# The order of seven products, four PSUM banks for them, and four banks for the second weight matrix

## The chip, the cores and the metric

The kernel runs as one program on one core of one Trainium2 chip. The metric is the device time of one execution in microseconds (us). The kernel is written with one instruction stream for each engine and with semaphores between them: TensorE (PE) multiplies, VectorE (DVE) and ScalarE (ACT) read the results in PSUM, GpSimd (POOL) works only in SBUF, and SyncE (SP) issues all DMAs. PSUM has 8 banks here, `ps[:, 0..7, :]`, each with room for 512 float32 values in a partition.

## The reference

One inference step of one layer. The stage that the change touches is the SwiGLU feed-forward at the end of the layer:

```python
def residual_tail(h, oa, ob, g_out_a, g_out_b, w_out, g_ffn, w_gate, w_up, w_down):
    mixed = jnp.concatenate([rmsnorm(oa, g_out_a), rmsnorm(ob, g_out_b)], axis=-1)
    h = h + mixed @ w_out
    u = rmsnorm(h, g_ffn)
    return h + (jax.nn.silu(u @ w_gate) * (u @ w_up)) @ w_down
```

There are 1024 prompt frames and 32 sample frames (1056 tokens), `D_MODEL` is 1024 and `D_FF` is 2816, which is 22 blocks of 128. All is float32. Ahead of this stage stand a combined input projection, two kinds of attention (forgetting attention and sliding-window attention) and the output projection; the change leaves those alone.

## The kernel before

**Three matmuls for one.** Each float32 matrix is kept as a high part (rounded to float32r) and a low part (the rest). `product` (L734 to L737) issues three matmuls: high by high (L735), weights high by data low (L736), weights low by data high (L737). For each operand ACT copies the high part and DVE subtracts to get the low part.

**Seven products for eight.** In the feed-forward the two matrices gate and up, and the two halves of the tokens, are treated as a 2 by 2 block product and computed with seven block products in place of eight (Strassen's scheme in Winograd's form). The weights' sums and differences are made by POOL (`weight_sums`, L2436 to L2451: four in each step), those of the input by `input_sum` once per pass, in place, in the staged columns `st_a` (pass 0, POOL) or `st_b` (pass 1, POOL and DVE). `fu0` to `fu6` are the seven inputs, each as `hi` and `lo`; `fw` has 9 slots for split weights.

**Passes and steps.** Pass 0 takes 512 tokens (halves of 256), pass 1 takes 544 (halves of 272). Each pass has 22 steps `g`, one for each 128 columns of `w_gate` and `w_up`; steps 0 to 21 are pass 0, steps 22 to 43 pass 1. `SETS` is 44 and `NF` 22. In a step PE issues products P0 to P6 (`ffn_product`, 12 matmuls each). Product number e = 7g + i is written to bank `e % SPARE`, and `SPARE` is 6. Between products stand the four pieces D0 to D3 of the product with `w_down` of the step before (`down_piece`): order P0 D0 P1 P2 D1 P3 P4 D2 P5 P6 D3. In pass 0 a piece is one group of 512 columns, in pass 1 two groups of 272. Groups go to banks 6 and 7 in turn, as `down_banks` (L445) lays out; the turned rows (`turn_half`, PE transposes of `y` for the output) use the same two.

**What DVE does with the products.** ACT copies P0 to `x1` (`copy_out`). DVE then has seven places in each step, at fixed points of its program, where it adds a bank (L2100 and L2109). Before the change they are: P1 to the first gate, P2 to `x2`, P4 to `x3`, P5 to the second gate, P3 to both `x2` and `x3` (`add_fourth`, L2102, two instructions), and, at the start of the next step, P6 to `x2`. In the text these are called place 1, place 2, place 3, place 4, the double place and place 6. Between them DVE splits weights (L2055), multiplies the gates (L2119), splits the hidden values (L2126) and `w_down` (L2134), and adds the groups of D0 to D3 to `y` (L2149, or L2146 in the first unit of a pass).

**What holds PE.** Before product e, PE waits (`bank_read`, L1136) until the product SPARE back has been read, that is for a place of DVE (or `f_x`, the copy by ACT). Before a group, it waits until the last user of its bank has been added (`down_bank_free`, L1163), until the hidden values are split (`f_hl`) and until the weights are (`dw_lo`). In steps 0 and 22 the inputs `fu` change too, so products wait for `u_lo`.

**The pass change.** In step 21 DVE and ACT also make the inputs of pass 1 (`input_hi`, `input_lo` L2084, `input_sum` L2074 to L2078), and in step 22 the last two of them. In steps 24 and 25 the first four result rows are turned and added to the residual (`add_half`, L2160); in steps 26 to 29 DVE normalises them (`out_row`, L2181, after the double place and ahead of place 6). The last units are computed after step 43, with the rows 4 to 8.

Of the kernel before, what the change touches and what calls it, by code (L numbers as in the profile page):

```python
# [421 lines left out]
U_ORDER = (0, 1, 2, 3, 5, 6, 4)  # L422
# [41 lines left out]
def build(nc, x_p, x_s, ck_fox, cv_fox, cl_fox, ck_swa, cv_swa, rel_bias, g_attn, w_in, b_forget, sinks,  # L464
# [17 lines left out]
    with ExitStack() as ctx:  # L482
# [231 lines left out]
        U_FROM = ((0, 0), (1, 0), (0, 0), (0, 1), (0, 1), (1, 1), (1, 0))  # L714
        U_SUMS = (0, 0, 2, 1, 4, 0, 3)
# [17 lines left out]
        def _(pe):  # L733
# [402 lines left out]
            def bank_read(g, i):  # L1136
# [3 lines left out]
                if i == 3:  # L1140
                    return S["f_p7"], 2 * g + 2
                return S["f_add"], 5 * g + {1: 1, 2: 2, 4: 3, 5: 4, 6: 5}[i]

            def ffn_product(g, i):
# [4 lines left out]
                if g % NF == 0:  # L1149
                    pe.wait_ge(S["u_lo"], 7 * p + U_ORDER.index(i) + 1)  # L1150
# [85 lines left out]
        def _(act):  # L1236
# [413 lines left out]
            for s in range(1, TILES + 1):  # L1650
# [11 lines left out]
                if s >= 6:  # L1662
                    for i in U_ORDER[2 * (s - 6):2 * (s - 6) + 2]:
# [6 lines left out]
            for g in range(SETS):  # L1670
                if g >= 1:
                    silu(g - 1, 1)
                if g == NF:
                    input_hi(1, 6)
                copy_out(g)
                if g == NF:
                    input_hi(1, 4)
# [20 lines left out]
                if g == NF - 1:  # L1698
                    input_hi(1, 5)
# [19 lines left out]
        def _(dve):  # L1719
# [343 lines left out]
            def input_sum(p, x):  # L2063
# [4 lines left out]
                else:  # L2068
                    dve.wait_ge(S["u_sum"], 4 * p + x)
                    dve.wait_ge(S["u_lo"], 7 * p + (1, 2, 4)[x - 1])  # L2070
# [6 lines left out]
                else:  # L2077
                    dve.tensor_tensor(b12, b22, b11, ALU.subtract).then_inc(S["u_sum"], 1)  # L2078

            def input_lo(p, i):  # L2080

                n = HALF_OF[p]
                dve.wait_ge(S["u_hi"], 7 * p + U_ORDER.index(i) + 1)
# [3 lines left out]
            def add_bank(g, i):  # L2087
# [4 lines left out]
                dst, src = {1: (gate0, first), 2: (x2, first), 4: (x3, x2), 5: (gate1, x3), 6: (x2, x2)}[i]  # L2092
# [3 lines left out]
                elif i < 6:  # L2096
                    dve.wait_ge(S["f_add"], 5 * g + i - 2)
# [4 lines left out]
            def add_fourth(g):  # L2102

                n, par = HALF_OF[pass_of(g)], g % 2
                dve.wait_ge(S["f_pe"], 7 * g + 4)
                for x in range(2):
                    dve.wait_ge(S["f_add"], 5 * g + 3 + x)
                    part = x23[par][:, x, 0:n]
                    dve.tensor_tensor(part, part, bank((7 * g + 3) % SPARE, n), ALU.add).then_inc(S["f_p7"], 1)  # L2109
# [75 lines left out]
            for s in range(1, TILES + 1):  # L2185
# [9 lines left out]
                if s >= 6:  # L2195
                    for i in U_ORDER[2 * (s - 6):2 * (s - 6) + 2]:
# [8 lines left out]
            for g in range(SETS):  # L2205
# [6 lines left out]
                if g == NF:  # L2212
                    input_lo(1, 6)
# [6 lines left out]
                if g == NF:  # L2220
                    input_lo(1, 4)
# [19 lines left out]
                if g == NF - 1:  # L2241
                    input_lo(1, 2)
                if g == NF + 2:
# [4 lines left out]
                add_bank(g, 4)  # L2248
# [3 lines left out]
                if g == NF - 1:  # L2252
                    input_lo(1, 3)
                    input_sum(1, 3)
# [590 lines left out]
```

## Time and profile before

| | us |
|---|---|
| median of three executions | 1372.18 |
| lowest, highest | 1371.8, 1377.6 |
| profiled execution, its own time | 1376.14 |
| its span | 1374.2 |
| PE busy | 1320.5 (96%) |
| DVE busy | 948.3 (69%) |
| ACT busy | 661.1 (48%) |
| POOL busy | 526.3 (38%) |

The span is the time from the first to the last instruction in the trace. A view of the trace gives places in it as microseconds from the span's start. In the page's row of 40 slices PE reads 9 nearly everywhere, and DVE reads 9 or 8 from the 26th slice on, which is the feed-forward; so the two engines run side by side there. Ends of matmuls are modelled, and a matmul's own 0.28 us overlaps with the next one's, so a product's length is read from start to start.

### The profile page before, as it was taken

What the parts mean: (1) busy time and instruction counts of PE and PEld (TensorE: products, weight loads), DVE (VectorE), ACT (ScalarE), POOL (GpSimd) and SP (SyncE); (2) the same over time, 40 slices, a digit from 0 to 9 for tenths busy, and PEclk for the clock granted to TensorE, in tenths of its full rate; (3) what the DMA queues carried; (4) which work ended last, traced back from release to release, by engine and by line L of the source; (5) the groups of instructions that cost most, each with busy time, mean ns of one, the idle gap of its engine ahead of it and who ended that gap; (6) DMA issues with size and microseconds to landing.
All of it is one profiled execution on the core that took longest, in us unless ns stands there. A gap on an engine that the chain in (4) does not pass through costs nothing.

```text
span 1374.2 us, 25904 instructions
## 1 busy us (share of the span) xinstructions
PE 1320.5 (96%) x9497; PEld 1198.1 (87%) x9497; DVE 948.3 (69%) x1899; ACT 661.1 (48%) x1418; POOL 526.3 (38%) x499
## 2 busy tenths in 40 slices
PE   7999999999999899999999999999999999999996
PEld 5989888788887678777999999998889999999996
DVE  6346653333232433478999999999998998899976
ACT  6346564756455553367443444445454433334432
POOL 3045552545435232125544444444343444434400
PEclk9999999999999999999999999999999999999999
DMA  7631115312112344563343333332532444333311
GB/s 207 109 81 36 33 52 162 101 32 63 63 45 78 96 170 137 172 207 107 94 122 108 93 106 111 103 98 81 166 92 78 124 124 155 96 105 93 93 51 65
DMA packets 167235, 141.10 MB, mean 103 GB/s; under 512 B 17280, under 2 KB 143328, under 8 KB 166600
## 3 DMA queue, kind: packets, MB, share of 16 engines
q1 hardware_dynamic: 167112, 139.46, 35.0%
q8 instruction: 77, 1.26, 0.4%
q14 instruction: 46, 0.38, 0.1%
HBM read 116.00 MB, written 23.54 MB: 102 GB/s over the span
## 4 chain that ended last, share of the span: by engine, by line
PE 80%; DVE 10%; issue 5%; ACT 3%; DMA 2%; POOL 1%; SPq 0%; DVEq 0%; ACTq 0%
PE ps L735 24%; PE ps L737 23%; PE ps L736 23%; PE ps L939 3%; DVE fw L2055 2%; PE ps L869 1%; DMA cb<-c_scratch 1%; PE ps L951 1%; PE ps L816 1%; PE ps L1028 1%; DVE y L2149 1%; PE ps L907 1%; DMA ob<-o_scratch 1%; DVE ps L1850 1%; DVE h_lo L2126 1%
## 5 line engine op out<-in xcount | busy, mean ns | idle before, releaser
L2446 POOL TENSOR_TENSOR sums<-fraw 128x512 f32<-128x512 f32 x44 | 73.3, 1666 | 402.8 <-DMA fraw<-in_w_up 381.3
L735 PE MATMUL ps<-h_hi,dw 128*128 128x272 f32 (+1 forms) x512 | 168.0, 328 | 8.9 <-DVE y L2149 6.4
L2055 DVE TENSOR_TENSOR fw<-sums,fw 128x512 fp32r<-128x512 f32 x176 | 172.5, 999 | 0.0
L2402 POOL TENSOR_TENSOR pl_x<-sp_x,ph_x 128x512 fp32r<-128x512 f32 (+5 forms) x120 | 102.3, 866 | 169.8 <-ACT sp_x L1428 168.5
L737 PE MATMUL ps<-h_hi,dw 128*128 128x272 f32 (+1 forms) x512 | 166.8, 326 | 0.0
L736 PE MATMUL ps<-h_lo,dw 128*128 128x272 f32 (+1 forms) x512 | 165.9, 324 | 0.0
L1632 ACT ACTIVATE sg<-sg 128x256 f32<-128x256 f32 (+1 forms) x88 | 37.5, 426 | 230.9 <-DVE sg L2100 230.6
L2149 DVE TENSOR_TENSOR y<-y,ps 128x272 f32<-128x272 f32 (+1 forms) x240 | 120.4, 516 | 25.0 <-PE ps L737 22.4
L1592 ACT ACTIVATE fw<-sums 128x512 fp32r<-128x512 f32 x176 | 104.5, 622 | 41.6 <-PE ps L737 39.2
L735 PEld LDWEIGHTS ps<-h_hi,dw 128*128 128x128 f32 x512 | 96.4, 188 | 15.2 <-issue 10.8
L1427 ACT ACTIVATE ph_x<-ps,negc 128x512 fp32r<-128x512 f32 (+5 forms) x120 | 63.0, 525 | 84.2 <-PE ps L951 84.2
L737 PEld LDWEIGHTS ps<-h_hi,dw 128*128 128x128 f32 x512 | 96.6, 189 | 7.2
L736 PEld LDWEIGHTS ps<-h_lo,dw 128*128 128x128 f32 x512 | 96.7, 189 | 3.9
L1592 ACT ACTIVATE fw<-fraw 128x512 fp32r<-128x512 f32 x132 | 78.3, 626 | 30.6 <-PE ps L737 30.6
L2055 DVE TENSOR_TENSOR fw<-fraw,fw 128x512 fp32r<-128x512 f32 x132 | 91.1, 717 | 0.0
L1884 DVE CUSTOM_DVE_ANT_0 ps<-ps,cb 128x512 f32<-128x512 f32 (+4 forms) x72 | 40.1, 597 | 71.1 <-PE ps L916 42.9
L2449 POOL TENSOR_TENSOR sums<-fraw 128x512 f32<-128x512 f32 x44 | 82.7, 1880 | 0.0
L2451 POOL TENSOR_TENSOR sums<-fraw,sums 128x512 f32<-128x512 f32 x44 | 78.6, 1787 | 0.0
L2134 DVE TENSOR_TENSOR dw<-draw,dw 128x1024 fp32r<-128x1024 f32 x43 | 78.4, 1822 | 0.0
L735 PE MATMUL ps<-u_hi,cw1hi 128*128 128x384 f32 (+1 forms) x216 | 75.4, 349 | 0.0
L735 PE MATMUL ps<-u_hi,cw0hi 128*128 128x384 f32 (+1 forms) x216 | 75.0, 347 | 0.0
L736 PE MATMUL ps<-u_lo,cw1hi 128*128 128x384 f32 (+1 forms) x216 | 70.0, 324 | 0.0
(358 smaller groups left out, 4428.7 us busy)
## 6 DMA issues: line engine op xcount, KB each, us to landing
fraw<-in_w_gate SPq DMA_DIRECT2D x44, 512.0 KB, 4.0
fraw<-in_w_up SPq DMA_DIRECT2D x44, 512.0 KB, 5.3
draw<-in_w_down SPq DMA_DIRECT2D x44, 512.0 KB, 3.6
x_scratch<-xb SPq DMA_DIRECT2D x16, 512.0 KB, 2.9
raw<-in_w_in SPq DMA_DIRECT2D x14, 512.0 KB, 4.0
cb<-c_scratch SPq DMA_DIRECT2D x4, 1312.0 KB, 7.2
xt<-in_x_prompt SPq DMA_DIRECT2D x8, 512.0 KB, 4.2
out<-outb SPq DMA_DIRECT2D x16, 256.0 KB, 3.1
```

Source lines behind the costliest of these rows:

```text
L735: pe.matmul(out, wh, xh, start=start, stop=False)
L736: pe.matmul(out, wh, xl, start=False, stop=False)
L737: return pe.matmul(out, wl, xh, start=False, stop=stop)
L1427: act.activation(ph_x[2 * (v % 2) + h][0:rows, 0:n], ps[0:rows, b + h, 0:n], ACT.Exp, bias=decay, scale=-1.0)
L1592: act.activation(fw[e % SLOTS][:, 0, :, :], weight_block(g, i), ACT.Copy).then_inc(S["fw_hi"], 1)
L2055: dve.tensor_tensor(lo, weight_block(g, i), hi.bitcast(F32), ALU.subtract).then_inc(S["fw_lo"], 1)
L2134: dve.tensor_tensor(down_weight(n)[:, 1, :, :], draw[:], down_weight(n)[:, 0, :, :].bitcast(F32), ALU.subtract)\
L2149: dve.tensor_tensor(dst, dst, bank(DOWN_BANK["group", at], width), ALU.add).then_inc(S["y_add"], 1)
L2402: pool.tensor_tensor(pl_x[at][0:rows, 0:n], sp_x[at][0:rows, 0:n], ph_x[at][0:rows, 0:n].bitcast(F32), ALU.subtract).then_inc(S["x_pl"], 1)
L2446: pool.tensor_tensor(s1, a21, a22, ALU.add).then_inc(S["fw_sum"], 1)
L2449: pool.tensor_tensor(s3, a11, a21, ALU.subtract).then_inc(S["fw_sum"], 1)
L2451: pool.tensor_tensor(s4, a12, s2, ALU.subtract).then_inc(S["fw_sum"], 1)
```

## The change

Three things are changed together.

1. The products P3, P4 and P5 are renumbered. What was P3 (added to both sums) is now P5; what was P4 is now P3, and what was P5 is now P4. So DVE's places are now: P1, P2, P3, P4, P5 (double, `add_both`), P6. The places themselves stay where they were in DVE's program, with the same operands and sizes.
2. `SPARE` goes from 6 to 4: products use banks 0 to 3. The groups and the turned rows use banks 4 to 7.
3. The inputs and weight sums follow the new numbers: `U_FROM`, `U_SUMS`, `SUM_OF`, `SUM_DONE`, `U_ORDER`, the order of two of POOL's four sums, and in step 21 the last `input_sum`, which stands ahead of `down_lo` now and not after the fourth input.

```diff
-SPARE = 6
+SPARE = 4
-SUM_OF = {2: 0, 3: 1, 4: 2, 5: 3}
-SUM_DONE = {2: 2, 3: 3, 4: 1, 5: 4}
+SUM_OF = {2: 0, 5: 1, 3: 2, 4: 3}
+SUM_DONE = {2: 2, 3: 1, 4: 3, 5: 4}
-U_ORDER = (0, 1, 2, 3, 5, 6, 4)
+U_ORDER = ((0, 1, 2, 4, 5, 3, 6), (0, 1, 2, 3, 4, 5, 6))
...
-            uses += [("turn", 4 + t, 6 + t % 2) for t in range(4)]
-        uses.append(("group", at, 6 if n == NF + 1 else 6 + at % 2))
+            uses += [("turn", 4 + t, 4 + t % 4) for t in range(4)]
+        uses.append(("group", at, 4 + at % 3 if n == NF + 1 else 4 + at % 4))
...
-        U_FROM = ((0, 0), (1, 0), (0, 0), (0, 1), (0, 1), (1, 1), (1, 0))
-        U_SUMS = (0, 0, 2, 1, 4, 0, 3)
+        U_FROM = ((0, 0), (1, 0), (0, 0), (0, 0), (1, 1), (0, 1), (1, 0))
+        U_SUMS = (0, 0, 2, 4, 0, 1, 3)
...
-                if i == 3:
+                if i == 5:
                     return S["f_p7"], 2 * g + 2
-                return S["f_add"], 5 * g + {1: 1, 2: 2, 4: 3, 5: 4, 6: 5}[i]
+                return S["f_add"], 5 * g + min(i, 5)
...
-                dst, src = {1: (gate0, first), 2: (x2, first), 4: (x3, x2), 5: (gate1, x3), 6: (x2, x2)}[i]
+                dst, src = {1: (gate0, first), 2: (x2, first), 3: (x3, x2), 4: (gate1, x3), 6: (x2, x2)}[i]
...
-            def add_fourth(g):
+            def add_both(g):
...
-                dve.wait_ge(S["f_pe"], 7 * g + 4)
+                dve.wait_ge(S["f_pe"], 7 * g + 6)
...
                 if g == NF - 1:
                     input_lo(1, 2)
+                    input_sum(1, 3)
...
-                add_bank(g, 4)
+                add_bank(g, 3)
...
                 if g == NF - 1:
                     input_lo(1, 3)
-                    input_sum(1, 3)
...
-                add_bank(g, 5)
-                add_fourth(g)
+                add_bank(g, 4)
+                add_both(g)
```

On PE nothing moves: the same matmuls stand in the same order, and only what they wait for differs. Here is P4 of step 2, its first matmul before (-) and now (+); `fw_186` is a weight slot, `f_add` counts places 1 to 4 and 6, and `f_x` the copies by ACT.

```order
 L736 MATMUL ps<-fu3lo,fw_195 128x256
 L737 MATMUL ps<-fu3hi,fw_195 128x256
-L735 MATMUL ps<-fu4hi,fw_186 128x256 [waits f_add,fw_lo]
+L735 MATMUL ps<-fu4hi,fw_186 128x256 [waits f_x,fw_lo]
 L736 MATMUL ps<-fu4lo,fw_186 128x256
 L737 MATMUL ps<-fu4hi,fw_186 128x256
```

P4 waited for the bank of the fifth product of the step before (place 4) and now waits for P0 of its own step. With `bank_read` worked out for all seven, P0 now waits for place 3 of the step before (it was place 1), P1 for place 4 (it was place 2), P2 for the double place (as before), P3 for place 6 (it was place 3), P4 for ACT's copy, P5 for place 1 and P6 for place 2 of its own step.

On PE again, a group of `w_down` in step 25, behind the four turned rows of that step; `e_r` counts the turned rows that DVE has added.

```order
 L736 MATMUL ps<-fu5lo,fw_186 128x272
 L737 MATMUL ps<-fu5hi,fw_186 128x272
-L735 MATMUL ps<-h_hi_190,dw_215 128x272 [waits y_add,dw_lo,f_hl]
+L735 MATMUL ps<-h_hi_190,dw_215 128x272 [waits e_r,dw_lo,f_hl]
 L736 MATMUL ps<-h_lo_191,dw_215 128x272
 L737 MATMUL ps<-h_hi_190,dw_215 128x272
```

This is the third group, behind P5, and the fourth has the same difference: it waited for the first group's addition and now waits for a turned row, since the four turned rows have four banks. The first two groups waited for the last two of the four turned rows of that step and now wait for the first two.

On DVE, in step 21 (the pass change), from the third input on; `fu2lo` to `fu5lo` are inputs of pass 1 and `st_b` the staged columns.

```order
 L2084 TENSOR_TENSOR fu2lo<-st_b,fu2hi 128x1088
+L2078 TENSOR_TENSOR st_b<-st_b 128x4x272
 L2134 TENSOR_TENSOR dw_216<-draw,dw_216 128x1024
 L2100 TENSOR_TENSOR x_1_221<-x_1_221,ps 128x256
 L2149 TENSOR_TENSOR y<-y,ps 128x512
 L2084 TENSOR_TENSOR fu3lo<-st_b,fu3hi 128x1088
-L2078 TENSOR_TENSOR st_b<-st_b 128x4x272
 L2055 TENSOR_TENSOR fw_213<-sums_217,fw_213 128x512
 L2055 TENSOR_TENSOR fw_192<-sums_217,fw_192 128x512
 L2100 TENSOR_TENSOR sg_214<-x_1_221,ps 128x256
```

The sum has moved ahead of four instructions, of which one is place 3 (the row of L2100 on `x_1`); the last row shown, L2100 on `sg`, is place 4. The number of instructions on each engine is the same.

## Rows read from the trace of the kernel before

**Rows 1.** The page: busy time of each engine, and the chain by engine.
```profile
PE 1320.5 (96%) x9497; PEld 1198.1 (87%) x9497; DVE 948.3 (69%) x1899; ACT 661.1 (48%) x1418; POOL 526.3 (38%) x499
...
PE 80%; DVE 10%; issue 5%; ACT 3%; DMA 2%; POOL 1%; SPq 0%; DVEq 0%; ACTq 0%
```

**Rows 2.** Stretches: length, busy of PE, PEld, DVE, ACT, POOL, clock, DMA, GB/s.
```profile
800.00:900.00 100.00, 100.00 (x706) 93.50 (x706) 91.82 (x151) 43.14 (x85) 44.43 (x26) 1.00 0.36 104
938.00:972.00 34.00, 30.05 (x192) 27.17 (x192) 33.69 (x44) 16.38 (x26) 11.39 (x7) 0.95 0.21 63
1023.29:1034.63 11.34, 9.71 (x75) 9.28 (x74) 8.43 (x15) 8.28 (x13) 5.63 (x4) 1.00 0.13 48
1051.26:1068.94 17.68, 16.85 (x134) 16.66 (x134) 16.81 (x30) 6.85 (x13) 6.76 (x4) 1.00 0.39 106
1051.26:1120.72 69.46, 67.29 (x530) 66.63 (x530) 64.95 (x114) 27.39 (x52) 27.23 (x16) 1.00 0.41 119
1203.83:1220.44 16.61, 16.61 (x134) 16.61 (x134) 15.22 (x27) 6.80 (x13) 6.67 (x4) 1.00 0.36 97
1344.87:1361.60 16.73, 15.02 (x113) 14.00 (x112) 11.43 (x22) 4.07 (x7) 0.00 (x0) 1.00 0.07 27
```

**Rows 3.** Waits of PE from 640 to 1374: total us, times, longest.
```profile
PE ps L735 <- DVE y L2149: 6.9, 8, 2.7
```

**Rows 4.** DVE in order of time, end of step 12: start, us, what.
```profile
815.05 0.41 DVE L2100 TENSOR_TENSOR x<-x,ps 128x256 f32<-128x256 f32 x1
...
818.50 0.41 DVE L2100 TENSOR_TENSOR sg<-x,ps 128x256 f32<-128x256 f32 x1
```

**Rows 5.** PE in order of time, products P0 and P1 of step 13.
```profile
818.29 0.28 PE L735 MATMUL ps<-fu0hi,fw 128*128 128x256 f32 x1
...
821.09 0.28 PE L735 MATMUL ps<-fu1hi,fw 128*128 128x256 f32 x1
```

**Rows 6.** DVE in order of time, end of step 1.
```profile
653.02 0.41 DVE L2100 TENSOR_TENSOR x<-x,ps 128x256 f32<-128x256 f32 x1
...
656.42 0.41 DVE L2100 TENSOR_TENSOR sg<-x,ps 128x256 f32<-128x256 f32 x1
```

**Rows 7.** PE in order of time, P1 and P2 of step 2.
```profile
654.42 0.28 PE L735 MATMUL ps<-fu1hi,fw 128*128 128x256 f32 x1
...
657.63 0.36 PE L735 MATMUL ps<-fu2hi,fw 128*128 128x256 f32 x1 [1.64 <-DVE x L2109]
```

**Rows 8.** DVE in order of time, the pass change (steps 21 and 22).
```profile
959.77 0.41 DVE L2100 TENSOR_TENSOR x<-x,ps 128x256 f32<-128x256 f32 x1
...
962.08 1.29 DVE L2078 TENSOR_TENSOR st_b<-st_b 128x1088 f32<-128x1088 f32 x1
...
964.49 0.42 DVE L2100 TENSOR_TENSOR sg<-x,ps 128x256 f32<-128x256 f32 x1
```

**Rows 9.** PE in order of time, the pass change: P0 of step 22, D0, P4.
```profile
956.56 0.29 PE L735 MATMUL ps<-fu0hi,fw 128*128 128x272 f32 x1
...
960.92 0.47 PE L735 MATMUL ps<-h_hi,dw 128*128 128x512 f32 x1 [2.68 <-DVE y L2149]
...
971.75 0.36 PE L735 MATMUL ps<-fu4hi,fw 128*128 128x272 f32 x1 [0.78 <-issue]
```

**Rows 10.** PE in order of time, second and third group of step 25.
```profile
1025.57 0.36 PE L735 MATMUL ps<-h_hi,dw 128*128 128x272 f32 x1 [1.34 <-DVE hrow L2160]
...
1028.36 0.36 PE L735 MATMUL ps<-h_hi,dw 128*128 128x272 f32 x1 [0.29 <-DVE y L2146]
```

**Rows 11.** PE in order of time, after step 43: groups at 1337 and the last turns.
```profile
1337.73 0.36 PE L735 MATMUL ps<-h_hi,dw 128*128 128x272 f32 x1 [0.83 <-DVE y L2149]
...
1362.08 2.84 PE L1204 MATMUL ps<-ident,y 128*128 128x128 f32 x24 [0.98 <-DVE y L2149]
```

**Rows 12.** DVE in order of time, one row of step 26 and one of the end.
```profile
1051.58 1.28 DVE L2181 SCALAR_TENSOR_TENSOR hrow<-hrow,small,g_fin 128x1024 f32<-128x1024 f32 x1
...
1341.49 1.22 DVE L2134 TENSOR_TENSOR dw<-draw,dw 128x1024 fp32r<-128x1024 f32 x1
```

More of the change, by code:

```diff
@@ L1149, in ffn_product @@
                 if g % NF == 0:
-                    pe.wait_ge(S["u_lo"], 7 * p + U_ORDER.index(i) + 1)
+                    pe.wait_ge(S["u_lo"], 7 * p + U_ORDER[p].index(i) + 1)
                 if e >= SPARE:
@@ L1662, in _ @@
                 if s >= 6:
-                    for i in U_ORDER[2 * (s - 6):2 * (s - 6) + 2]:
+                    for i in U_ORDER[0][2 * (s - 6):2 * (s - 6) + 2]:
                         input_hi(0, i)
@@ L1673, in _ @@
                 if g == NF:
-                    input_hi(1, 6)
+                    input_hi(1, 5)
                 copy_out(g)
                 if g == NF:
-                    input_hi(1, 4)
+                    input_hi(1, 6)
                 if g == NF - 1:
@@ L1698, in _ @@
                 if g == NF - 1:
-                    input_hi(1, 5)
+                    input_hi(1, 4)
                 if g == NF + 3:
@@ L2069, in input_sum @@
                     dve.wait_ge(S["u_sum"], 4 * p + x)
-                    dve.wait_ge(S["u_lo"], 7 * p + (1, 2, 4)[x - 1])
+                    dve.wait_ge(S["u_lo"], 7 * p + x)
                 if x == 0:
@@ L2095, in add_bank @@
                     dve.wait_ge(S["f_x"], g + 1)
-                elif i < 6:
-                    dve.wait_ge(S["f_add"], 5 * g + i - 2)
+                elif i < 5:
+                    dve.wait_ge(S["f_add"], 5 * g + i - 1)
                 else:
@@ L2108, in add_fourth @@
                     part = x23[par][:, x, 0:n]
-                    dve.tensor_tensor(part, part, bank((7 * g + 3) % SPARE, n), ALU.add).then_inc(S["f_p7"], 1)
+                    dve.tensor_tensor(part, part, bank((7 * g + 5) % SPARE, n), ALU.add).then_inc(S["f_p7"], 1)
             def gated(g, j):
@@ L2195, in _ @@
                 if s >= 6:
-                    for i in U_ORDER[2 * (s - 6):2 * (s - 6) + 2]:
+                    for i in U_ORDER[0][2 * (s - 6):2 * (s - 6) + 2]:
                         input_lo(0, i)
@@ L2212, in _ @@
                 if g == NF:
-                    input_lo(1, 6)
+                    input_lo(1, 5)
                 weights_lo(g, 0)
@@ L2220, in _ @@
                 if g == NF:
-                    input_lo(1, 4)
+                    input_lo(1, 6)
                 pieces_added(g, 0)
@@ L2265, in _ @@
                 if g == NF - 1:
-                    input_lo(1, 5)
+                    input_lo(1, 4)
                 if g == NF + 4:
@@ L2439, in weight_sums @@
                 a22 = fraw[g % 2][:, 1, 4:8, :]
-                s1, s2, s3, s4 = (sums[g % 2][:, SUM_OF[i], :, :] for i in (4, 2, 3, 5))
+                s1, s2, s3, s4 = (sums[g % 2][:, SUM_OF[i], :, :] for i in (3, 2, 5, 4))
                 pool.wait_ge(S[f"fw_in{g % 2}"], 32 * (g // 2 + 1))
@@ L2459, in input_sum @@
                     pool.wait_ge(S["u_sum"], 4 * p + x)
-                    pool.wait_ge(S["u_lo"], 7 * p + (1, 2, 4)[x - 1])
+                    pool.wait_ge(S["u_lo"], 7 * p + x)
                 if x == 0:
```

8 lines of the change are left out of this document (4 added, 4 removed).

## The prediction, made before the changed kernel ran

> **What bounds the kernel now.** I read the page first: PE is busy for 1320.5 us and the chain that ends last is PE for 80% of the span and DVE for 10% [rows 1]. Then the view of stretches over the feed-forward. In a stretch of pass 0 PE is busy for all of its 100 us and DVE for 91.8, and in a step of pass 1 (16.61 us) PE again for all of it and DVE for 15.22 [rows 2]. So in the steady steps PE sets the pace, and what the change does there can only add. In a few stretches PE has gaps: at the pass change (30.05 busy of 34.00), in step 25 (9.71 of 11.34), in steps 26 to 29, and after the last step (15.02 of 16.73) [rows 2]. Third, the view of waits says what PE waited for: most of all additions to `y`, 6.9 us in 8 waits [rows 3]. An addition to `y` frees a bank of a group, and there are two of those. A gain can come only from these gaps. Last, I laid the starts of products beside the ends of DVE's places, since with four banks each product waits for a later place than before.
>
> **Steady steps: cost nothing.** P0 now waits for place 3 of the step before, P1 for place 4. Place 3 of step 12 ends at 815.05 + 0.41 = 815.46 and P0 of step 13 starts at 818.29; place 4 ends at 818.91 and P1 starts at 821.09 [rows 4, 5]. The margins are 2.8 and 2.2 us. P2 waits for the double place as before, and P3 to P6 wait for places that lie further ahead of them. The additions keep their sizes and their places in DVE's program, and each now reads a product that PE finishes at the same point or earlier, the double place apart: its product is P5 now, which ends a product and a group (together 2.80, the distance of the two rows in [rows 5]) ahead of P0's 818.29, at 815.5, well before the double place, which stands behind place 4. So: 0, and upwards whatever a DVE that runs over 2.2 us later would cost (the second rival).
>
> **The start: +0.3.** In the first steps DVE is far behind, since there is no `w_down` work on PE yet. Place 3 of step 1 ends at 653.43 and place 4 at 656.83 [rows 6]. P1 of step 2 started at 654.42, which is now too early by 2.4 us: it starts at about 656.9, and P2 a product (1.4 us, half of that 2.80) later, at 658.3, in place of 657.63, where P2 already ended a wait of 1.64 us for the double place [rows 7]. So most of the new wait takes the place of an old one, and 0.7 is left. Against it, step 0 gets shorter, because the input that is split last is now needed by P6 and no longer by P4, and with it step 1 on DVE can start a little earlier. No row prices that. Ends: -0.5 and +1.5; I take +0.3, near the 0.7 of the rows.
>
> **The pass change: +0.1.** This is the place where the change bites. P0 of step 22 started at 956.56, and place 3 of step 21 stood at 959.77, with the last sum of 1.29 us behind it at 962.08 [rows 8, 9]. The sum is now ahead of place 3, so place 3 ends at 959.77 + 1.2 + 0.4 = 961.4, and P0 starts there, 4.9 us later than before. But D0 behind it was waiting until 960.92 anyway (2.68 us, for an addition to `y` that now has a bank of its own), and P4 waited until 971.75 for the input that DVE split last [rows 9]; that input now belongs to P6. From 961.5 on PE has P0, D0, P1, P2, D1, P3 ahead of P4: four products of 12 x 0.126 = 1.51 (the pace is worked out under step 25) and two groups of 1.38, 8.8 us, so P4 could start at 970.3, and with P1 held until place 4 (964.49 + 0.42 = 964.9 [rows 8]) at 970.8, 1 us early. The clock takes that back. The stretch from 938 to 972 has a mean of 0.95 of the full clock [rows 2], which is 34 x 0.05 / 0.5 = 3.4 us at the lower of the two levels, 1.2 GHz. The same 3.4 us now lie wholly on PE's work, and cost 1.7 us, less the 0.5 that P1 would have waited: P4 at 972.0 and so +0.1 against 971.75 or a little more. Ends: -1.0 (no low stretch on the path) and +1.8 (a second low stretch of that length, as PE's gap grows from 2.7 to about 5 us).
> The Trainium skill (TensorE: Matmul & The Clock Gate, HAM oscillation) says that PE falls back to the half clock after it has stood idle, so a longer gap can cost a second low stretch. By that rule the sum would end 1.7 us higher. The trace agrees that one such stretch follows the gap; how it is with a longer gap no row here shows.
>
> **Step 25: -2.3.** Behind the four turned rows the second group waited 1.34 us for the last turned row's addition and the third another 0.29 [rows 10]. With four banks it is the fourth group that needs the last turned row's bank; it comes a product and three groups after the first, at 1023.29 + 1.51 + 2.27 = 1027.1, and the addition was over at 1025.57. The stretch from 1023.29 to 1034.63 then has only its 72 matmuls. A steady step holds 132 in 16.61 us, 0.126 each, so 72 take 9.06 us and not 11.34 [rows 2]: -2.3. Ends: 0 (DVE gives nothing back) and -2.3.
>
> **Steps 26 to 29: -3.0.** In each of these DVE has a row of the result of 1.28 us ahead of place 6 [rows 12], and with it the additions of D3 come late; D0 of the next step needed their bank. The four steps take 69.46 us, the first of them 17.68 [rows 2]. Four steady steps are 66.44. With four banks D0 waits for D2 of the step before, which DVE adds ahead of place 4 and so before its result row. What is late next is place 3 for P0, and that stands ahead of the result row too. DVE itself has 64.95 us of work in these four steps [rows 2], under 66.44, so it can follow. Ends: 0 and -3.0.
>
> **After step 43: -2.8.** The third group there waited for an addition to `y`, and started at 1337.73 and not at once, 1.0 us late [rows 11]. Then DVE splits the last part of `w_down` until 1341.49 + 1.22 = 1342.7 [rows 12]; the ninth group needs it and started at 1344.87, since groups were held by two banks on the way. It can start at 1342.9, -2.0. From there PE had 16.73 us, with 15.02 busy, DVE 11.43 [rows 2]: 1.7 us of gaps, which two more banks close, but for what DVE's last additions and two result rows hold up; I take half, -0.8. Sum -2.8. The last turns, at 1362.08 [rows 11], and all behind them move along. Ends: -1.0 (only the first wait) and -3.1.
>
> **Other edits: 0.** POOL's two sums are exchanged; POOL mostly waits for weights, with 44.43 us busy of 100 [rows 2]. ACT makes the fourth input later in step 21, as it now needs the last sum, but DVE has `w_down`, place 3 and an addition between that sum and its own part of that input. The DMAs are the same.
>
> **Sum.** 0 + 0.3 + 0.1 - 2.3 - 3.0 - 2.8 = -7.7. On the profiled execution's own 1376.14 us that is 1368.4. That execution is 4.0 us above the median of the three runs, 1372.18, and nothing in the page says why; I take the difference off the median: 1364.5 us.
>
> **Rivals.**
> 1. *DVE takes the gain back.* In pass 1 with four banks PE is no longer held at D0, but DVE was busy for 16.81 us in step 26, more than the 16.61 of a steady step [rows 2]. If it is the true bound of steps 25 to 29, the 5.3 us there are not gained but wait at a later product. For it: DVE's busy time. Against: 64.95 in four steps, and the gaps of DVE in step 25 (8.43 busy of 11.34 [rows 2]). Then -2.4, 1369.8 us.
> 2. *Four product banks are too few* (the other side). The margin of P1 is 2.2 us in the steady steps [rows 4, 5]. If DVE, with a different meeting of its splits with POOL's sums, runs later than that, P1 waits in each step; decided from a lag of 2.2 us on. By 0.5 us in each of the 37 steps outside the places above it is +18.5, with the gains 1383. For it: DVE is busy 91.8% [rows 2]. Against: it has 8% to catch up with, and steps of equal work have had that margin.
> 3. *The two bad places cost their full price:* the start +1.5, the pass change +1.8 with a second low stretch and a P0 that no longer hides behind D0. Then 1364.5 + 2.9 = 1367.4.
> 4. *The new order does more:* the start -0.5, the pass change -1.0, the end -3.1: 1362.3. It goes with the forecast.
>
> **How the numbers follow.** Forecast (with 4): 0.65; rival 1: 0.16; rival 3: 0.14; rival 2: 0.05. 0.5% is about what a measurement of this kernel can tell from no change, 6.9 us: faster means under 1365.3. The forecast's own range is 1361.5 to 1366.5, since medians of three runs scatter too, and about 0.83 of it lies under 1365.3: faster 0.54 and 0.11 of it the same; rivals 1 and 3 are the same but for 0.01: same 0.41; slower 0.05. The range of 8 in 10 takes in most of rivals 1 and 3: 1361.5 to 1370.
>
> **What would show it.** The waits of PE for `y` go from 6.9 us to below 1; steps 26 to 29 take 16.6 us each; the stretch of step 25 takes about 9; the waits that appear are for place 4 in step 2 and for place 3 in step 22, of some 5 us; the span from the first turn after the last group to the end stays as it is. Wrong would be: products that wait in steady steps, a DVE without gaps in steps 25 to 30, or more than one low stretch of the clock near 961.

## The result, and the profile after

The changed kernel took 1367.74 us (median of 8 runs, 1366.13 to 1370.4), the kernel before in the same comparison 1375.62 us (8 runs, 1371.8 to 1379.0). The ratio is 0.9947 with a 95% interval from 0.9933 to 0.996: 7.3 us faster (7.9 by the two medians). The prediction was 1364.5 us, as 7.7 us less than a base of 1372.18 us.

The page of the changed kernel, busy time and chain, answers to [rows 1]:

```profile
PE 1316.1 (96%) x9497; PEld 1197.0 (88%) x9497; DVE 944.3 (69%) x1899; ACT 660.2 (48%) x1418; POOL 520.9 (38%) x499
...
PE 84%; DVE 8%; issue 3%; ACT 3%; DMA 2%; POOL 1%; SPq 0%; DVEq 0%; ACTq 0%
```

PE has 84% of the chain where it had 80%. Its span is 1364.3 us. Then the stretches that answer to [rows 2], with the same columns (length, busy of PE, PEld, DVE, ACT, POOL, clock, DMA, GB/s): a steady stretch of pass 0, the pass change, step 25 from its first group on, step 26, steps 26 to 29, and the end from the ninth group behind D3 to the last addition to `y`.

```profile
800.00:900.00 100.00, 100.00 (x704) 93.43 (x703) 90.89 (x154) 45.63 (x89) 40.97 (x25) 1.00 0.38 106
938.00:972.00 34.00, 28.89 (x189) 26.72 (x189) 33.69 (x49) 18.32 (x30) 8.68 (x5) 0.95 0.27 74
1020.61:1029.69 9.08, 9.08 (x74) 9.08 (x73) 8.46 (x15) 8.28 (x13) 5.79 (x4) 1.00 0.21 61
1046.33:1062.95 16.62, 16.62 (x134) 16.62 (x133) 15.50 (x31) 6.96 (x14) 6.32 (x4) 1.00 0.43 128
1046.33:1112.77 66.44, 66.44 (x530) 66.44 (x529) 61.51 (x116) 27.56 (x53) 26.10 (x16) 1.00 0.44 128
1334.91:1350.46 15.55, 13.96 (x114) 13.63 (x112) 11.68 (x24) 4.06 (x7) 0.00 (x0) 1.00 0.07 29
```

The reader is to see where PE's gaps went. Step 25 has 9.08 us and not 11.34, steps 26 to 29 have 66.44 and not 69.46, both without a gap. The pass change still has one (28.89 busy of 34.00), and so has the end (13.96 of 15.55).

What PE waits for, in the changed kernel from 630 us on (total us, times, longest), answers to [rows 3]:

```profile
PE ps L735 <- DVE x L2100: 6.1, 2, 5.1
PE ps L1204 <- DVE y L2149: 2.1, 1, 2.1
PE ps L735 <- DVE sg L2100: 1.9, 2, 1.7
```

No group waits for an addition to `y` any more (before: 6.9 us in 8 waits). Place 3 (`x`: P0 of step 22 with 5.1 us, and P0 of step 2 with 1.0) and place 4 (`sg`: P1 of step 2 with 1.7) have taken their stead, and the last turns wait 2.1 us.

Laid beside each other from the first product of the feed-forward (P0 of step 0) to the end, the two profiled executions differ as follows. The last column is the changed kernel profiled a second time, `c1_changed_again`, told of below.

| stretch | predicted | changed | again |
|---|---|---|---|
| ahead of P0 of step 0 | | -3.3 | -3.5 |
| start (to P0 of step 3) | +0.3 | +0.8 | +1.9 |
| steps 3 to 20 | 0 | 0.0 | 0.0 |
| pass change (P0 of step 21 to P0 of step 23) | +0.1 | +0.1 | +1.1 |
| steps 23 and 24 | 0 | -0.2 | -0.5 |
| step 25 | -2.3 | -2.2 | -2.2 |
| steps 26 to 29 | -3.0 | -3.0 | -3.0 |
| steps 30 to 42 | 0 | 0.0 | 0.0 |
| end (from P0 of step 43) | -2.8 | -2.0 | -3.3 |
| from P0 of step 0 on | -7.7 | -6.5 | -5.9 |

The first row lies ahead of all that was changed: in all twelve other profiled executions of this study P0 of step 0 came 1.3 to 3.5 us earlier than in the one of before, `e4_before_rows_later`, which has the same order and banks, among them (1.8 us). So it is taken to be the execution's and not the change's.

### The profile page after: what moved, and what is told of

The parts are those of the page before. It is cut to its first block, busy times and chain, and to the rows that moved or that the text cites. A ratio compares the mean times of both kernels' runs of the same rounds, so it can differ in the third digit from the quotient of the medians.

```text
span 1364.3 us, 25904 instructions
## 1 busy us (share of the span) xinstructions
PE 1316.1 (96%) x9497; PEld 1197.0 (88%) x9497; DVE 944.3 (69%) x1899; ACT 660.2 (48%) x1418; POOL 520.9 (38%) x499
## 3 DMA queue, kind: packets, MB, share of 16 engines
q8 instruction: 78, 1.28, 0.4%
## 4 chain that ended last, share of the span: by engine, by line
PE 84%; DVE 8%; issue 3%; ACT 3%; DMA 2%; POOL 1%; SPq 0%; DVEq 0%; ACTq 0%
PE ps L735 25%; PE ps L737 24%; PE ps L736 24%; PE ps L939 3%; DVE fw L2055 2%; PE ps L869 1%; DMA cb<-c_scratch 1%; PE ps L951 1%; PE ps L816 1%; PE ps L1028 1%; PE ps L907 1%; DVE ps L1850 1%; DMA ob<-o_scratch 1%; ACT sp_x L1428 0%; ACT raw L1551 0%
## 5 line engine op out<-in xcount | busy, mean ns | idle before, releaser
L2446 POOL TENSOR_TENSOR sums<-fraw 128x512 f32<-128x512 f32 x44 | 72.0, 1636 | 402.5 <-DMA fraw<-in_w_up 397.8
L2055 DVE TENSOR_TENSOR fw<-sums,fw 128x512 fp32r<-128x512 f32 x176 | 175.0, 1013 | 0.0
L2055 DVE TENSOR_TENSOR fw<-fraw,fw 128x512 fp32r<-128x512 f32 x132 | 89.7, 706 | 0.0
L2451 POOL TENSOR_TENSOR sums<-fraw 128x512 f32<-128x512 f32 x44 | 78.8, 1790 | 0.0
L2134 DVE TENSOR_TENSOR dw<-draw,dw 128x1024 fp32r<-128x1024 f32 x43 | 75.6, 1757 | 0.5 <-ACT dw L1617 0.5
L736 PE MATMUL ps<-u_lo,cw0hi 128*128 128x384 f32 (+1 forms) x216 | 69.7, 323 | 0.0
```

Source lines behind the costliest of these rows:

```text
L736: pe.matmul(out, wh, xl, start=False, stop=False)
L2055: dve.tensor_tensor(lo, weight_block(g, i), hi.bitcast(F32), ALU.subtract).then_inc(S["fw_lo"], 1)
L2134: dve.tensor_tensor(down_weight(n)[:, 1, :, :], draw[:], down_weight(n)[:, 0, :, :].bitcast(F32), ALU.subtract)\
L2446: pool.tensor_tensor(s1, a21, a22, ALU.add).then_inc(S["fw_sum"], 1)
L2451: pool.tensor_tensor(s3, a11, a21, ALU.subtract).then_inc(S["fw_sum"], 1)
```

## The experiments

Times are medians; the kernel before ran in each comparison (1375.38 us with the first four, 1374.71 with the next four, 1375.29 with the last three). Single steps are read from one profiled execution of each kernel.

**e1_old_order_4_4**: the banks of the change with the old order of products.

```diff
-SPARE = 6
+SPARE = 4
-            uses += [("turn", 4 + t, 6 + t % 2) for t in range(4)]
-        uses.append(("group", at, 6 if n == NF + 1 else 6 + at % 2))
+            uses += [("turn", 4 + t, 4 + t % 4) for t in range(4)]
+        uses.append(("group", at, 4 + at % 3 if n == NF + 1 else 4 + at % 4))
```

> The order of before with the banks of the changed kernel (four for products, four for groups and turned rows). Theory (the new order is what makes four product banks enough): P0 now needs the bank of the old P3, which is read at the double place, after P5. In the trace of before the double place of step 12 ends at 819.57 and P0 of step 13 starts at 818.29, so it comes 1.3 us too late there; by the margins of P2 over the double place (2.9 to 4.1 us in pass 0, 4.1 to 5.0 in pass 1, where P2 stands 4.2 and 4.5 us behind P0) the shortfall is 0.1 to 1.3 us a step in pass 0 and 0 to 0.4 in pass 1: some 12 + 3 us lost, 8 won by the groups' banks, so about 7 us slower than before (3 to 12), and PE waits for the double place in most steps of pass 0. Rival (four product banks do in any order, all that matters is the banks of the groups): 7 us faster than before, as the changed kernel.

Measured: 1412.63 us, ratio 1.0269 (1.0247 to 1.0291), 37 us slower. Its waits of PE:

```profile
PE ps L735 <- DVE x L2109: 36.0, 28, 8.1
PE ps L1204 <- DVE y L2149: 2.1, 1, 2.1
```

The wait for the double place (L2109) is there as the theory had it, 28 times, but the price was five times too small. It is not a shortfall paid once in a while: it closes a loop. Step 13 of that kernel starts at 835.36. Here are place 1 and the double place of DVE in it, and P0 of step 14:

```profile
839.85 0.42 DVE L2100 TENSOR_TENSOR sg<-x,ps 128x256 f32<-128x256 f32 x1 [0.72 <-PE ps L737]
...
851.17 0.74 DVE L2109 TENSOR_TENSOR x<-x,ps 128x256 f32<-128x256 f32 x2
```
```profile
852.06 0.36 PE L735 MATMUL ps<-fu0hi,fw 128*128 128x256 f32 x1 [1.11 <-DVE x L2109]
```

P0 waits for the double place of the step before, that stands 12 us behind place 1 in DVE's program (839.85 to 851.91), and place 1 waits for PE's P1 (0.72 us in its row), which follows P0. Between the two DVE has no pause. Once PE is late, place 1 is late, and with it the double place and the next P0: the step takes the time round the loop, here 4.49 us from P0 to place 1, 12.06 in DVE's program and 0.15 back to P0, together 16.70. Over steps 4 to 19 it is 16.73 us a step (P0 of step 4 at 685.22, of step 20 at 952.95) and not 15.35 (680.16 and 925.71 before). So the four product banks cost 1.4 us in each of these steps in the old order and nothing in the new one.

**e2_new_order_6_2** and **e3_new_order_4_2**: the new order with six and two banks, and with four and two (two of the eight then unused). The edit of e2 against the changed kernel; e3 leaves `SPARE` at 4 and has the rest:

```diff
-SPARE = 4
+SPARE = 6
-            uses += [("turn", 4 + t, 4 + t % 4) for t in range(4)]
-        uses.append(("group", at, 4 + at % 3 if n == NF + 1 else 4 + at % 4))
+            uses += [("turn", 4 + t, 6 + t % 2) for t in range(4)]
+        uses.append(("group", at, 6 if n == NF + 1 else 6 + at % 2))
```

> The new order with the banks of before (six and two). Theory (the gain is in the groups' banks): the waits for y at steps 25 to 30 and after step 43 are all there, so step 25 takes 11.3 us for its stretch, steps 26 to 29 lose 3.0; time as before, within 2 us (the start about 0.5 less, the pass change 0 to 1 more since D2 of step 21 is added later). Rival (the order carries a good part): 3 us or more faster than before.

> The new order with four product banks, and groups and turned rows in two banks as before (two banks stand empty). Theory: +0.8 us at the start and +1 or less at the pass change against before, none of the gains of step 25, of steps 26 to 29 and of the end: 1 to 2 us slower than before, 8 to 9 slower than the changed kernel. Rival (fewer product banks cost nothing, since the waits hide each other): as before, within 0.5 us.

Measured: 1372.58 us, ratio 0.9988 (0.9975 to 1.0001), and 1375.37 us, ratio 0.9999 (0.9989 to 1.0009). The waits of PE for `y` in e2 and in e3:

```profile
PE ps L735 <- DVE y L2149: 7.6, 7, 4.1
```
```profile
PE ps L735 <- DVE y L2149: 3.9, 6, 0.9
```

Neither has the gains of steps 25 to 29 (together +0.4 and 0.0 us against before) nor that of the end. The whole gain of the changed kernel hangs on the four banks for groups. The order by itself (e2) gains nothing that can be told from none: its interval reaches from 3.4 us faster to no change, and its profiled execution is 0.6 us longer than before from P0 of step 0 on. What it does is to make these banks free at no price. For e3, 1 to 2 us slower than before was expected. Its profiled execution has the two costs (+0.8 us at the start, +1.3 at the pass change), but the medians show no difference.

**e4_before_rows_later**: the kernel before, with the result rows of steps 26 to 29 moved behind the additions of D3.

```diff
                     add_piece(g - 2, 3)
+                if NF + 5 <= g < NF + 9:
+                    out_row(g - NF - 5)
...
-                if NF + 4 <= g < NF + 8:
-                    out_row(g - NF - 4)
```

> The kernel before with only DVE's four normalised result rows (L2181 in steps 26 to 29) moved behind place 6 and the additions of D3, into the next step. Theory (D0 waits in steps 27 to 30 because the row stands ahead of D3's additions, and nothing else on DVE is late): the four steps take 66.5 us and not 69.5, 3.0 us faster than before, with two banks. Rival (DVE has too much work in these steps): the wait moves to another place and the four steps stay above 68.5 us.

Measured: 1371.37 us, ratio 0.9981 (0.9971 to 0.999). Steps 26 to 29 lose 3.0 us, what the change gave them. So it was DVE's result row ahead of these additions that held the two banks, and a move of four instructions gets this term without any bank. It also gives a like for the end, below.

**e5_end_rows_later**: the changed kernel, with result rows 7 and 8 behind the last addition to `y`.

```diff
-                if k in (20, 22):
-                    out_roots(ROWS[k // 2 - 6], 1)
-                    out_row(ROWS[k // 2 - 6])
+            for t in (7, 8):
+                out_roots(t, 1)
+                out_row(t)
```

> The changed kernel with the normalised result rows 7 and 8 (the last two L2181 ahead of the last additions) moved behind the last addition to y, ahead of row 4. In the trace of the changed kernel PE is done with the last group at 1348.7 and the last turns start at 1350.96, as DVE spends two rows of 1.28 us (1347.21, 1349.28) ahead of its last addition; then the clock is at its lower level and the 24 turns take 4.51 us and not 2.84. Theory (DVE's rows hold the last turns, and the gap brings the low clock): the turns start 1.4 us earlier relative to the last group, the gap of 2.1 us falls below 1, and the kernel is 1.3 to 2.5 us faster than the changed kernel. Rival (the tail is DVE's own work, which only changes its order): the rows of 4 to 6 move back by as much, and the time is that of the changed kernel, within 0.5 us.

Measured: 1366.0 us, ratio 0.9934 (0.992 to 0.9949). DVE and PE at the end of the changed kernel, and then of e5:

```profile
1347.21 1.29 DVE L2181 SCALAR_TENSOR_TENSOR hrow<-hrow,small,g_fin 128x1024 f32<-128x1024 f32 x1
...
1349.28 1.27 DVE L2181 SCALAR_TENSOR_TENSOR hrow<-hrow,small,g_fin 32x1024 f32<-32x1024 f32 x1
...
1350.48 0.42 DVE L2149 TENSOR_TENSOR y<-y,ps 128x272 f32<-128x272 f32 x1
1352.89 1.22 DVE L2167 TENSOR_TENSOR hrow<-hrow,ps 128x1024 f32<-128x1024 f32 x1 [1.99 <-PE ps L1204]
```
```profile
1350.96 4.51 PE L1204 MATMUL ps<-ident,y 128*128 128x128 f32 x24 [2.08 <-DVE y L2149]
```
```profile
1350.46 0.44 DVE L2149 TENSOR_TENSOR y<-y,ps 128x272 f32<-128x272 f32 x1 [0.31 <-PE ps L737]
1351.00 1.28 DVE L2181 SCALAR_TENSOR_TENSOR hrow<-hrow,small,g_fin 128x1024 f32<-128x1024 f32 x1
1352.38 1.27 DVE L2181 SCALAR_TENSOR_TENSOR hrow<-hrow,small,g_fin 32x1024 f32<-32x1024 f32 x1
1353.58 3.46 DVE L2167 TENSOR_TENSOR hrow<-hrow,ps 128x1024 f32<-128x1024 f32 x3
```
```profile
1350.95 2.84 PE L1204 MATMUL ps<-ident,y 128*128 128x128 f32 x24 [0.53 <-DVE y L2149]
```

In the changed kernel the two rows stand between DVE and the last addition, and PE has been idle for 2.08 us by its row when the turns start. In e5 the gap is 0.53, and the same 24 turns take 2.84 us and not 4.51. From P0 of step 43 to the end e5 takes 51.0 us and the changed kernel 52.1. That looked like a gain of 1.1 us; c1 shows below what it is.

**e6_sum_after_place3**: the changed kernel, with the sum of step 21 behind place 3 and the split of the fourth input behind that of the weights.

```diff
                     input_lo(1, 2)
-                    input_sum(1, 3)
...
                 add_bank(g, 3)
+                if g == NF - 1:
+                    input_sum(1, 3)
...
+                weights_lo(g, 3)
                 if g == NF - 1:
                     input_lo(1, 3)
-                weights_lo(g, 3)
```

> The changed kernel with the last sum of the inputs (L2078) of step 21 right behind place 3, and the fourth input's low part behind the two weight splits, so that DVE does not wait for ACT. Theory (P0 of step 22 waits for place 3 of step 21 and for nothing else): P0 starts 1.2 us earlier than the 959.1 of the changed kernel, relative to P0 of step 21; place 4 stays, so P1 gains less than that, and P5 of step 22 0 to 1.2 us. Rival (the low clock follows PE's gap at whatever point it starts, and takes the same from the products): P5 of step 22 within 0.3 us of the changed kernel.

Measured: 1365.22 us, ratio 0.9927 (0.9915 to 0.9939). P0 of step 22 in the changed kernel, and then in e6:

```profile
959.12 0.57 PE L735 MATMUL ps<-fu0hi,fw 128*128 128x272 f32 x1 [5.11 <-DVE x L2100]
```
```profile
958.32 0.36 PE L735 MATMUL ps<-fu0hi,fw 128*128 128x272 f32 x1 [3.71 <-DVE x L2100]
```

The wait shrinks by 1.4 us, about the sum's 1.29, and the pass change takes 1.06 us less than in the changed kernel; it does so in e8 and in its repeat as well (0.9 and 1.1 us less). The clock does not explain it: in e6 the low stretch (959.1 to 962.5) lies wholly behind P0's start and so on PE's work, in the changed kernel only 2.9 us of it do.

**e7_banks_5_3**: five banks for products, three for groups and turns, in both passes.

```diff
-SPARE = 4
+SPARE = 5
-            uses += [("turn", 4 + t, 4 + t % 4) for t in range(4)]
-        uses.append(("group", at, 4 + at % 3 if n == NF + 1 else 4 + at % 4))
+            uses += [("turn", 4 + t, 5 + t % 3) for t in range(4)]
+        uses.append(("group", at, 5 + at % 2 if n == NF + 1 else 5 + at % 3))
```

> The changed kernel with five banks for products and three for groups and turned rows. Theory (each side needs only what its slack says): P0 waits for place 2 and P1 for place 3, so P0 of step 22 does not wait and its gap goes to D0 or P1; with three banks D0 of steps 27 to 30 waits for the third group back, which is added in time, so steps 26 to 29 stay at 16.6 us; step 25 loses about 1 us since its fourth group needs the first one's bank; in all within 1 us of the changed kernel. Rival (any bank fewer for the groups brings the waits back): 2 us or more slower than the changed kernel.

Measured: 1366.22 us, ratio 0.9936 (0.9922 to 0.995). It wins 2.5 us at the start and 0.7 at the pass change against the changed kernel and gives back 1.4 us in step 25, 0.7 in steps 26 to 29, where it was expected to lose nothing, and 0.7 at the end. So three banks for groups are too few in all three places, and the fifth product bank helps in pass 0. Not all of the 2.5 is the bank's: DVE's place 3 of step 1 came 1.1 us earlier in this execution than in the changed kernel (21.7 and 22.8 us behind P0 of step 0), as it also did in e5, which has the changed kernel's banks. The pair c2 and e9, below, in which DVE runs alike there, puts the bank at 1.4.

**e8_both_moves**: the moves of e5 and e6 together.

> The changed kernel with both moves of DVE's work: result rows 7 and 8 behind the last addition, and the last sum behind place 3. If the two are independent, the sum of what each gains alone: 1.3 to 2.5 and 0 to 1.2 us, so 1.3 to 3.7 us faster than the changed kernel; if the tail is DVE's own work and the clock takes the rest, no gain.

Measured: 1365.02 us, ratio 0.9924 (0.9909 to 0.9938). By the ratios that is some 3 us under the changed kernel, inside the 1.3 to 3.7 expected, but its interval reaches that of the changed kernel (from 0.9933), and the two stand in different comparisons; the next one has both.

**c1_changed_again**, **c2_both_moves_again** (the changed kernel and e8, not edited) and **e9_five_then_four** (e8 with five and three banks in pass 0, four and four in pass 1), in one comparison. The edit of e9 against e8:

```diff
+def product_bank(e):
+    return e % 5 if e < 7 * NF else (e - 7 * NF) % 4
...
-        uses.append(("group", at, 4 + at % 3 if n == NF + 1 else 4 + at % 4))
+        uses.append(("group", at, 5 + at % 3 if n < NF else 4 + at % 3 if n == NF + 1 else 4 + at % 4))
```

> The changed kernel once more, in the same comparison as the next two, so that they can be set against it directly. Against the kernel before 7 to 8 us shorter, as the first time (7.3 us by the medians). If the first comparison owed part of its gain to the 3.3 us by which its first product came early, it should come out nearer 4 us. The stretch from the first product to the end should lose the same 2.2 us in step 25, 3.0 us in steps 26 to 29 and about 2 us behind the last step.

> The kernel with both moves once more (the two output rows behind the last add of y; the column sum of step 21 behind place 3). If the two gains seen in the single kernels (1.1 us at the end, 1.4 us at the change of pass) are real and add, it is 1.5 to 3 us shorter than the changed kernel in this comparison. If they were variation of the start and of the loads, it is within 1 us of it. At the end no stretch of the lower clock should begin at the last turns.

> Both moves, and five banks for products with three for groups in pass 0, four and four in pass 1. The theory that the fifth bank helps only where products wait for VectorE (the first steps, the change of pass) and the fourth group bank only from step 25 on makes it about 2 us shorter than the kernel with both moves: the start gains as with five and three (2.5 us there), and step 25 and steps 26 to 29 lose nothing. The rival, that the start with five banks came early only by the variation of 1 us and more that the start shows between runs, or that VectorE ends last at the change of pass whatever the banks, has it within 1 us of that kernel.

Measured: c1 1367.35 us, ratio 0.9943 (0.9927 to 0.9959); c2 1365.29, ratio 0.993 (0.9913 to 0.9947); e9 1363.99, ratio 0.9919 (0.9904 to 0.9934). The gain of the change repeats: 7.9 us. c2 is 2.1 us under c1 by the medians, as expected, though the intervals overlap. e9 is the fastest kernel of the study, 11.3 us under before and 3.4 under c1; over c2 it wins 1.3 us where 2 were expected, and its intervals don't tell it from c2. Its trace has the two halves of the expectation: the start 1.4 us shorter than in c2, step 25 and steps 26 to 29 with their full -2.2 and -3.0. Its pass change is 0.7 us longer than c2's, with the low clock for 6.8 us there and not 3.4.

What c1 overturned is the reading of e5. PE's last turns in c1:

```profile
1352.71 2.84 PE L1204 MATMUL ps<-ident,y 128*128 128x128 f32 x24 [2.08 <-DVE y L2149]
```

The same kernel, the same gap of 2.08 us, and this time the turns take 2.84 us. From P0 of step 43 to the end c1 takes 50.8 us, e5 51.0. So with turns of the same length, moving the two rows gained nothing: the turns start 1.25 us earlier, and DVE then has the two rows (1.28 and 1.27) to do ahead of the additions that follow. What it may save is the slow turns. They came in four of the five executions with the long gap (the changed kernel, e1, e6 and e7, but not c1), in two of the four with a gap of 1.0 us (e3 and e4, but not before and e2) and in none of the four with the short one (e5, e8, c2, e9). One execution of each kernel is too few to call that a rule.

## Why the prediction was right, and where it was off

**Steady steps: right.** Against P0 of step 3, no product of steps 3 to 20 moved by more than 0.01 us, nor did one of steps 31 to 42 against P0 of step 31, in the changed kernel and in c1, which have four banks for products and four for groups. e1 shows that the new order is the reason, and that the second rival (a product that waits in each step) was a real danger of four banks: 37 us, more than the 18.5 that it was priced at, since it was priced as a shortfall and not as a loop. What protected the kernel was the margins of 2.8 and 2.2 us in the prediction.

**Start: +0.3 predicted, +0.8.** P1 of step 2 waits for place 4, as said. PE's row in the changed kernel:

```profile
653.70 0.36 PE L735 MATMUL ps<-fu1hi,fw 128*128 128x256 f32 x1 [1.71 <-DVE sg L2100]
```

The 0.7 of the rows was the right size, and the 0.4 that I took off it for a shorter step 0 did not come: place 1 of step 1 stood 0.6 us earlier behind P0 of step 0 than before (15.2 and 15.8), but place 2 and all behind it did not (20.1 and 20.0). The term is not one number. The six executions with this start (the changed kernel, c1, e5, e6, e8, c2) have 0.0 once, 0.8 three times and 1.9 twice, so two lie past the +1.5 of the prediction, and e4, where nothing was changed there, has +1.0. The cause is an encounter of DVE with POOL in step 1. DVE and POOL in the changed kernel, and then in c1:

```profile
647.75 0.68 DVE L2055 TENSOR_TENSOR fw<-sums,fw 128x512 fp32r<-128x512 f32 x1
```
```profile
647.81 1.76 POOL L2446 TENSOR_TENSOR sums<-fraw 128x512 f32<-128x512 f32 x1 [1.20 <-DMA fraw<-in_w_up]
```
```profile
647.62 1.81 DVE L2055 TENSOR_TENSOR fw<-sums,fw 128x512 fp32r<-128x512 f32 x1
```
```profile
647.58 1.30 POOL L2446 TENSOR_TENSOR sums<-fraw 128x512 f32<-128x512 f32 x1 [1.11 <-DMA fraw<-in_w_up]
```

Whichever of the two starts second takes some 0.5 (POOL) or 1.1 us (DVE) longer, and here 0.06 us ahead or 0.04 behind decide, by when a load of weights lands. Set like against like, the term is +0.8 (the changed kernel and before, both with 0.68 for this split) and +0.9 (c1 and e4, with 1.81 and 1.77). In e5, the 0.0, POOL's sum waited for its load until 650.60, when this split had long been done; steps 3 and 4 then gave 0.2 back.

**Pass change: +0.1 predicted, +0.1.** P0 of step 22 starts behind place 3, at 959.12, which is 961.67 when shifted by the 2.55 us that the changed kernel is ahead; predicted 961.4. P4 starts at 969.32, so 971.87; predicted 972.0. In c1 the third rival's second stretch of low clock is there. The pass change in the changed kernel and in c1:

```profile
948.00:972.00 24.00, 18.89 (x118) 17.35 (x118) 23.79 (x33) 10.87 (x19) 6.47 (x4) 0.93 0.22 61
```
```profile
948.00:972.00 24.00, 18.89 (x115) 17.29 (x114) 23.79 (x31) 10.87 (x19) 7.26 (x4) 0.86 0.16 49
```

And in e4, where the stretch holds the same gap of PE as before (2.69 us there, 2.68 before):

```profile
948.00:972.00 24.00, 18.48 (x123) 16.62 (x123) 23.79 (x31) 10.85 (x18) 7.39 (x4) 1.00 0.12 39
```

The mean clock of 0.93 is 24 x 0.07 / 0.5 = 3.4 us at 1.2 GHz, and 0.86 is 6.7, at the same wait of 5.11 us. The longer one cost 1.0 us more, less than the 1.7 priced. The clock was low from 958.6 to 962.0 in the changed kernel, where P0 starts at 959.12, and from 958.4 to 965.2 in c1, where it starts at 960.14. So 2.9 and 5.1 us of it lay on PE's work: 2.2 more at half speed, 1.1 us. Of the executions with the changed kernel's program up to this point, the changed kernel and e5 have the short stretch and c1 has the long one, and e3, with the same order and product banks and a wait of 4.96 us, has the long one too. So the chance of 0.14 for that rival was low for this one part of it; the end +1.8 held. The low stretch of before, on the other hand, had cost nothing: e4, with the order of before, has none, and P4 of step 22 stands where it stood before (30.7 us behind P0 of step 21).

The Trainium skill (TensorE: Matmul & The Clock Gate, HAM oscillation) has PE fall back to the half clock after it stood idle. The rows of the changed kernel and of c1 agree, but the length of the gap does not settle how long: the same 5.11 us gave both, and behind 2.7 us the kernel before had 3.4 us at the lower clock and e4 none.

**Step 25: -2.3 predicted, -2.2. Steps 26 to 29: -3.0, -3.0.** Both mechanisms hold: e2 and e3 lose them with two banks, e7 loses 1.4 and 0.7 us of them with three, and e4 gets the second by moving DVE's row. The first rival, that DVE takes the gain back, falls with the full -2.2 and -3.0, and DVE was busy for 61.51 us of the 66.44, in the stretches above, after 64.95 in 69.46 before [rows 2]. DVE's costliest groups in these four steps whose mean changed most, before and then after:

```profile
L2134 DVE TENSOR_TENSOR dw<-draw,dw 128x1024 fp32r<-128x1024 f32 x4 | 8.2, 2040 | 0.0
...
L2126 DVE TENSOR_TENSOR h_lo<-sg,h_hi 128x272 fp32r<-128x272 f32 x8 | 6.8, 850 | 0.0
```
```profile
L2134 DVE TENSOR_TENSOR dw<-draw,dw 128x1024 fp32r<-128x1024 f32 x4 | 6.0, 1489 | 0.0
...
L2126 DVE TENSOR_TENSOR h_lo<-sg,h_hi 128x272 fp32r<-128x272 f32 x8 | 3.4, 430 | 0.0
```

The same twelve instructions took 15.0 us and then 9.4; 1.2 us of that came back in the splits of sums (L2055, 15.3 and 16.5). Three of the eight `h_lo` before took 1.5 us and not 0.43, each with a sum of POOL begun 0.1 to 0.2 us ahead of it. Here is the first, DVE and then POOL:

```profile
1060.98 1.53 DVE L2126 TENSOR_TENSOR h_lo<-sg,h_hi 128x272 fp32r<-128x272 f32 x1
```
```profile
1060.77 1.44 POOL L2446 TENSOR_TENSOR sums<-fraw 128x512 f32<-128x512 f32 x1 [11.50 <-DMA fraw<-in_w_up]
```

In the changed kernel none of the eight had a sum begun ahead of it. So at least 5.6 us of the busy time of these twelve was time in which DVE was held up, and busy time was no measure of its work.

**End: -2.8 predicted, -2.0, and -3.3 in c1.** In both executions the turns started 3.3 us earlier (38.7 us behind P0 of step 43, 42.0 before), more than the 2.8. The ninth group behind D3 came 2.0 us earlier, as predicted, but PE's own pace set it and not DVE's split, which was over at 1334.25 when the group started at 1334.91. The stretch from there to the turns lost 1.2 and not 0.8. That all behind the turns moves along, as the prediction has it, was so in c1: 12.1 us from their start to the end, as before. It was not so in the changed kernel's first execution, with 13.4 us, since the turns ran at the lower clock there. In front of them PE's wait grew from 0.98 us [rows 11] to 2.08, because the last group now ends while DVE is at its two result rows. That the slow turns are a matter of the execution, and do not need this wait, is seen in e4, the kernel before with four rows moved, and in e3, both at a gap of 0.99 us. Here are their rows, e4 first, and then the clock of e4 (0.79) and of before (1.00) from 1356 to 1364:

```profile
1358.23 4.51 PE L1204 MATMUL ps<-ident,y 128*128 128x128 f32 x24 [0.99 <-DVE y L2149]
```
```profile
1362.30 4.51 PE L1204 MATMUL ps<-ident,y 128*128 128x128 f32 x24 [0.99 <-DVE y L2149]
```
```profile
1356.00:1364.00 8.00, 5.49 (x30) 5.06 (x30) 5.53 (x8) 2.36 (x4) 0.00 (x0) 0.79 0.25 84
```
```profile
1356.00:1364.00 8.00, 5.81 (x45) 5.14 (x44) 5.85 (x12) 2.02 (x5) 0.00 (x0) 1.00 0.24 82
```

With the slow turns on both sides the end gains 3.2 us (52.1 in the changed kernel and 55.3 in e4), without them on both sides 3.3 (50.8 in c1 and 54.05 before). So the term was 0.5 us too small, and the single comparison of two profiles hid it.

**The sum and the base.** -7.7 was predicted for the difference, and 7.3 and 7.8 us came in two comparisons by the ratios (7.9 and 7.9 by the medians). That the sum is so close is in part luck: the start was 0.5 us worse than its term and the end 0.5 us better, like against like. The time itself, 1364.5, was 3.2 us too low, and that is the base: I took the profiled execution's 1376.14 us for 4.0 too slow because three runs had a median of 1372.18. In the comparisons the kernel before had medians of 1374.7 to 1375.6. The profiled execution was the better base; the three runs were on the fast side.

**The signs named ahead.** The waits for `y` are gone, the four steps take 16.6 us each, the stretch of step 25 takes 9.08, and the two waits that were named came. Two signs went the other way in one execution each: the time from the turns to the end grew by 1.3 us in the first, and c1 had the long low stretch near 961.

What is not settled: why steps 23 and 24 differ by 1.2 us between executions of kernels that are the same there (-0.6 against before in e6 and +0.7 in e8). The rows there show the same kind of encounter of DVE with POOL, but I did not trace each one. And nothing here tells why the low clock takes 3.4 us in one execution and 6.7 in the next.

## What to carry to other kernels

When a buffer rotation is cut, go round the loop that the new wait closes (this engine, the consumer's place, what its operands wait for, back to this engine) and compare the loop with the step: here a loop longer by 1.4 us cost 1.4 us in every step, while a margin of 2 us cost nothing. Banks are worth having where the consumer is late in bursts, and the cheaper cure may be to move the consumer's unrelated instruction behind the release (e4: 3.0 us for four instructions moved). And before a gain of a microsecond is read off two profiles, profile the unchanged kernel twice, since encounters of two engines and the clock move single stretches by as much.

## What the runs showed of the hardware that was not expected

- The 24 last turns took 2.84 us or 4.51 us for the same kernel, behind the same 2.08 us of idle PE. At a gap of 0.53 us they took 2.84 us in e5, and none of the four kernels with that gap had the low clock there; at 0.99 us (e3, e4) they were slow, at 0.98 (before [rows 11], e2) they were not.
- Two instructions of DVE and POOL that start within 0.1 us of each other: the later one is held up, DVE's split 1.81 us and not 0.68, POOL's sum 1.76 and not 1.30. A load that lands 0.1 us sooner can so cost 1.1 us. At 0.03 us or less between the two starts, either of them was the one held up.
